# Expert loop of a 256-token mixture of experts on one core: the gather turned round, and TensorE's work behind the first layer in another order

## The reference, cut to what matters

```python
def moe_ffn(h, router_w, router_b, w1, b1, w2, b2):
    ...
    logits = (xt @ router_w + router_b).astype(jnp.float32)
    top_v, top_e = lax.top_k(logits, TOP_K)
    gate = jax.nn.softmax(top_v, axis=-1)
    ...
    def expert_block(args):
        rows, e = args
        xb = xt[rows]
        hb = xb @ w1[e] + b1[e]
        g, u = hb[:, :D_EXPERT], hb[:, D_EXPERT:]
        g = jnp.minimum(g, SWIGLU_LIMIT)
        u = jnp.clip(u, -SWIGLU_LIMIT, SWIGLU_LIMIT)
        glu = g * jax.nn.sigmoid(g * SWIGLU_ALPHA)
        return ((u + 1.0) * glu) @ w2[e] + b2[e]
    ...
    out = jnp.zeros((N, D), y.dtype).at[row_tok].add(y * row_w[:, None].astype(y.dtype))
```

## Time and profile before

| | us |
|---|---|
| Runs of the kernel before, three | 2416.95, 2409.55, 2408.04 |
| Their median | 2409.55 |
| Span of the profiled execution | 2412.2 |
| First-layer biases of expert 0 to the end of the last output sums | about 465 to 1620 |
| Main passes, further passes in it | 32, 2 |

### The profile page before, as it was taken

The page is one execution under the profiler, slowest core; times in us unless marked ns, Lnnn a source line. Parts: engine busy times, 40 slices in busy tenths (PEclk is TensorE's granted clock), DMA queues, the critical chain, the costliest instruction groups (busy, mean ns, idle before and its releaser), DMA issues.

```text
span 2412.2 us, 31828 instructions
## 1 busy us (share of the span) xinstructions
PE 2198.9 (91%) x11682; PEld 1314.5 (54%) x11683; DVE 723.1 (30%) x1577; ACT 476.3 (20%) x969; POOL 0.2 (0%) x4
## 2 busy tenths in 40 slices
PE   6999989788989988898988889989999999989997
PEld 3767756433333333333333333336648995756996
DVE  1313223211111111111111111121426772643776
ACT  1222230111001001111001100011224542113553
POOL 0000000000000000000000000000000000000000
PEclk9999989889999999999999999999999999999999
DMA  9234571789938999999999957985317655532662
GB/s 338 84 128 175 209 214 36 306 310 373 365 140 349 376 383 380 375 387 390 378 382 373 384 228 317 352 309 149 102 32 201 186 165 139 140 119 66 188 193 79
DMA packets 225825, 591.02 MB, mean 245 GB/s; under 512 B 14603, under 2 KB 114498, under 8 KB 189796
## 3 DMA queue, kind: packets, MB, share of 16 engines
q1 hardware_dynamic: 223804, 587.69, 67.5%
q10 hardware_dynamic: 1960, 2.46, 0.3%
HBM read 587.48 MB, written 2.62 MB: 245 GB/s over the span
## 4 chain that ended last, share of the span: by engine, by line
PE 89%; ACT 4%; DVE 3%; issue 2%; DMA 1%; SPq 0%; ACTq 0%; DVEq 0%
PE psum L1682 20%; PE psum L1700 12%; PE psum L1814 10%; PE psum L1350 7%; PE psum L1659 5%; PE psum L1826 5%; PE psum L1451 5%; PE psum L1456 4%; PE psum L1713 3%; PE psum L1483 2%; ACT upper L1132 2%; PE psum L1430 2%; PE psum L1676 2%; DMA lower<-in_mod_w 1%; PE psum L1436 1%
## 5 line engine op out<-in xcount | busy, mean ns | idle before, releaser
L1682 PE MATMUL psum<-lower,upper 128*64 128x512 f32 x2176 | 490.7, 609 | 0.0
L1682 PEld LDWEIGHTS psum<-lower,upper 128*64 128x64 f32 x2176 | 155.2, 139 | 334.9 <-issue 334.9
L1700 PE MATMUL psum<-upper 128*64 128x512 f32 x1088 | 279.0, 671 | 14.1 <-issue 12.7
L1814 PEld LDWEIGHTS psum<-rounded 128*128 128x128 f32 x2112 | 258.6, 189 | 3.4
L1814 PE MATMUL psum<-rounded 128*128 128x256 f32 x2112 | 260.1, 283 | 0.0
L2270 DVE TENSOR_SCALAR upper<-psum 128x512 f32<-128x512 f32 x34 | 23.5, 691 | 743.5 <-PE psum L1682 743.5
L1700 PEld LDWEIGHTS psum<-upper 128*64 128x64 f32 x1088 | 97.3, 153 | 169.0 <-issue 167.1
L1350 PE MATMUL psum<-upper,lower 128*128 128x256 f32 (+1 forms) x944 | 171.1, 383 | 1.4 <-DVE upper L1918 1.4
L1350 PEld LDWEIGHTS psum<-upper,lower 128*128 128x128 f32 (+1 forms) x944 | 133.8, 169 | 34.5 <-issue 8.5
L1138 ACT ACTIVATE upper<-upper 128x512 f32<-128x512 f32 x34 | 21.4, 629 | 599.5 <-DVE upper L2270 599.5
L1659 PEld LDWEIGHTS psum<-upper 128*128 128x128 f32 x1056 | 122.0, 194 | 27.8 <-issue 24.3
(11 more groups left out here) (365 smaller groups left out, 1827.9 us busy)
## 6 DMA issues: line engine op xcount, KB each, us to landing
lower<-in_exp_w SPq DMA_DIRECT2D x256, 1024.0 KB, 9.5
upper<-in_exp_w SPq DMA_DIRECT2D x256, 512.0 KB, 6.3
lower<-in_ffn_w_up SPq DMA_DIRECT2D x88, 512.0 KB, 5.4
lower<-in_mod_w SPq DMA_DIRECT2D x12, 2048.0 KB, 10.5
lower<-in_w_in SPq DMA_DIRECT2D x12, 2048.0 KB, 10.4
lower<-in_ffn_w_down SPq DMA_DIRECT2D x44, 512.0 KB, 5.7
lower<-in_odd_w_in SPq DMA_DIRECT2D x8, 2048.0 KB, 11.8
lower<-in_even_w_in SPq DMA_DIRECT2D x7, 2048.0 KB, 12.8
```

The lines of the kernel that those rows point to most:

```text
L1682: ins = pe.matmul(bank[4 + r // 2][64 * half:64 * half + 64], xg[:, k, 0:SLOTS], w1[k][:, 512 * r:512 * r + 512], start=False, stop=(n == ...
L1700: ins = pe.matmul(bank[6][64 * half:64 * half + 64], hiddenT[:, k % 4, 64 * (k // 4):64 * (k // 4) + 64], w2[k][:, 512 * half:512 * half + ...
L1814: ins = pe.matmul(bank[4 + b][:, T * g:T * g + T], w[:, g, k, :], x[:, k, :], start=(k == m == 0), stop=(k == KD - 1 and m == 2))
```

## The change

Ahead of the loop the scaled and shifted tokens `h2T` (features by tokens) are turned back into `h2` (tokens by features), which takes the place of `xn2`: 16 transposes on TensorE and four copies on ScalarE, and two busy-keeping matmuls in place of four. The gather takes the 64-column selection as stationary operand and `h2` as moving one: four matmuls of 512 columns, two column halves at a time, into bank 6. Its result is slots by features; ScalarE copies it to `xg` (one copy), four transposes (`turn_gathered`) put it into bank 7, and VectorE copies it to `xgT` (one copy). Scale and shift are in `h2` already, so the copies have none. `turn_hidden` of the main pass goes to bank 6.

On TensorE the order behind the first layer becomes: wait for `y_ready`; gather; spread out; (wait for the clipping) slot info; (wait for `xg`) turn hidden; turn gathered; output sums. The wait for `y_ready` at the head of an expert is gone. A further pass gathers from `h2`, and one VectorE copy replaces its multiply and add.

```diff
-        xgT = arena.take(1024, P)
+        xgT, xg = arena.take(512), arena.take(512)
...
-        select = arena.take(NT * P, P)
+        select = arena.take(NT * SLOTS, SLOTS)
...
+            for i in range(NT):
+                for half in range(2):
+                    act.wait_ge(x2_turned, 4 + 2 * i + half + 1)
+                    act.activation(h2[:, i, 512 * half:512 * half + 512], bank[2 + 2 * i + half],
+                                   ACT.Copy).then_inc(h2T_act, 1)
...
                 act.wait_ge(gathered, n)
-                for k in range(4):
-                    ins = act.activation(xgT[:, k, :], bank[7][:, P * k:P * k + P], ACT.Identity,
-                                         scale=scale2[:, k:k + 1], bias=mod[:, 24 + k:25 + k])
-                ins.then_inc(xg_lo, 1)
+                act.activation(xg, bank[6], ACT.Copy).then_inc(xg_copied, 1)
...
-            keep_busy(bank[7], 4)
+            for i in range(NT):
+                for half in range(2):
+                    for k in range(4):
+                        ins = pe.transpose(bank[2 + 2 * i + half][:, P * k:P * k + P],
+                                           h2T[:, 4 * half + k, P * i:P * i + P], ident)
+                    ins.then_inc(x2_turned, 1)
+            keep_busy(bank[7], 2)
...
             def gather(n):
                 pe.wait_ge(select_ready, n)
-                for k in range(KD):
-                    for i in range(NT):
-                        ins = pe.matmul(bank[7 - k // 4][:, P * (k % 4):P * (k % 4) + P], xn2[:, i, P * k:P * k + P],
-                                        select[:, i, :], start=(i == 0), stop=(i == NT - 1))
+                for i in range(NT):
+                    for half in range(2):
+                        ins = pe.matmul(bank[6][64 * half:64 * half + 64], select[:, i, :],
+                                        h2[:, i, 512 * half:512 * half + 512], start=(i == 0), stop=(i == NT - 1),
+                                        tile_position=(0, 64 * half))
                 ins.then_inc(gathered, 1)
+
+            def turn_gathered(n):
+                pe.wait_ge(xg_copied, n)
+                for j in range(4):
+                    ins = pe.transpose(bank[7][:, P * j:P * j + P], xg[:, P * j:P * j + P], ident)
+                ins.then_inc(xg_turned, 1)
...
-                pe.wait_ge(xg_lo, e + 1)
-                pe.wait_ge(xg_hi, e + 1)
+                pe.wait_ge(xgT_ready, e + 1)
                 pe.wait_ge(main_steps["slot_data"], e + 1)
-                if not first:
-                    pe.wait_ge(y_ready, e)
...
                 if not first:
+                    pe.wait_ge(y_ready, e)
+                gather(e + 2)
+                if not first:
                     pe.wait_ge(spread_ready, e)
                     spread_out(y_ready, e, spreadT, y_sb, spread_done)
-                gather(e + 2)
-                pe.wait_ge(xg_lo, e + 2)
-                turn_hidden(hidden_ready, e + 1, hidden_turned)
+                pe.wait_ge(main_steps["clipped"], e + 1)
                 slot_info(bank[5], select, info_done)
-                pe.wait_ge(xg_hi, e + 2)
+                pe.wait_ge(xg_copied, e + 2)
+                turn_hidden(bank[6], hidden_ready, e + 1, hidden_turned)
+                turn_gathered(e + 2)
                 output_sums(hiddenT_ready, e + 1, e, w2_used)
...
             def copy_gathered(n):
-                dve.wait_ge(gathered, n)
-                for k in range(4, KD):
-                    ins = dve.tensor_scalar(xgT[:, k, :], bank[6][:, P * (k - 4):P * (k - 4) + P], scale2[:, k:k + 1],
-                                            mod[:, 24 + k:25 + k], ALU.mult, ALU.add)
-                ins.then_inc(xg_hi, 1)
+                dve.wait_ge(xg_turned, n)
+                dve.tensor_copy(xgT, bank[7]).then_inc(xgT_ready, 1)
...
-                    dve.tensor_tensor(xgT_ov, bank[7].rearrange("p (k s) -> p k s", k=KD),
-                                      scale2.rearrange("p (k o) -> p k o", o=1).to_broadcast(wide),
-                                      ALU.mult).then_inc(more_steps["scaled"], 1)
-                    dve.wait_ge(more_steps["scaled"], n)
-                    dve.tensor_tensor(xgT_ov, xgT_ov, mod[:, 24:32].rearrange("p (k o) -> p k o", o=1).to_broadcast(wide),
-                                      ALU.add)
+                    dve.tensor_copy(xgT_ov.rearrange("p k s -> p (k s)"), bank[7])
...
                 make_select(e + 1, select_ready)
                 activation(w1_used, gate_ready, tanh_ready, hidden_ready, main_steps, e + 1, e * KD + KD)
-                copy_gathered(e + 2)
...
                 dve.tensor_copy(slot_data, bank[5][:, 0:2]).then_inc(main_steps["slot_data"], 1)
+                copy_gathered(e + 2)
```

More of the change, by code:

```diff
@@ L667, in program @@
         main_steps = {n: sem("dve_" + n) for n in ("clipped", "up_times_gate", "slot_data")}
-        more_steps = {n: sem("dve_more_" + n) for n in ("clipped", "up_times_gate", "slot_data", "scaled")}
+        more_steps = {n: sem("dve_more_" + n) for n in ("clipped", "up_times_gate", "slot_data")}
         moe_out_ready = sem("moe_out_ready")
@@ L1666, in slot_info, with hidden_sums @@
                     for i in range(NT):
-                        ins = pe.matmul(o[SLOTS * half:SLOTS * half + SLOTS, 0:2], sel[:, i, 0:SLOTS], expert_data[:, i, :],
+                        ins = pe.matmul(o[SLOTS * half:SLOTS * half + SLOTS, 0:2], sel[:, i, :], expert_data[:, i, :],
                                         start=(i == 0), stop=(i == NT - 1), tile_position=(0, SLOTS * half))
                 ins.then_inc(done, 1)
-            def hidden_sums(xg, e, used=None):
+            def hidden_sums(rows_of, e, used=None):
                 pe.wait_ge(b1_in, 16 * e + 16)
@@ L1681, in hidden_sums @@
                         half = r % 2
-                        ins = pe.matmul(bank[4 + r // 2][64 * half:64 * half + 64], xg[:, k, 0:SLOTS],
+                        ins = pe.matmul(bank[4 + r // 2][64 * half:64 * half + 64], rows_of(k),
                                         w1[k][:, 512 * r:512 * r + 512], start=False, stop=(n == KD - 1),
@@ L1687, in hidden_sums, with turn_hidden @@
                 return ins
-            def turn_hidden(ready, n, done):
+            def turn_hidden(o, ready, n, done):
                 pe.wait_ge(ready, n)
                 for j in range(4):
-                    ins = pe.transpose(bank[7][:, P * j:P * j + P], hidden[:, P * j:P * j + P], ident)
+                    ins = pe.transpose(o[:, P * j:P * j + P], hidden[:, P * j:P * j + P], ident)
                 ins.then_inc(done, 1)
@@ L1715, in spread_out, with gathered_rows @@
                 ins.then_inc(done, 1)
+            def gathered_rows(k):
+                at = P * (k % 4) + 64 * (k // 4)
+                return xgT[:, at:at + SLOTS]
             pe.wait_ge(route_ready, 1)
+            pe.wait_ge(h2T_act, 8)
             gather(1)
             slot_info(bank[5], select, info_done)
+            turn_gathered(1)
             def expert(e, first=False):
@@ L1735, in further_pass @@
                     pe.wait_ge(ov["select"], n)
+                    if p == 1 and not first:
+                        pe.wait_ge(y_ready, e)
                     for k in range(KD):
                         for i in range(NT):
-                            pe.matmul(bank[7][:, SLOTS * k:SLOTS * k + SLOTS], xn2[:, i, P * k:P * k + P],
+                            pe.matmul(bank[7][:, SLOTS * k:SLOTS * k + SLOTS], h2[:, i, P * k:P * k + P],
                                       select_ov[:, i, :], start=(i == 0), stop=(i == NT - 1))
@@ L1741, in further_pass @@
                     pe.wait_ge(ov["xg"], n)
-                    hidden_sums(xgT_ov, e).then_inc(ov["hidden"], 1)
-                    turn_hidden(ov["act"], n, ov["turned"])
+                    hidden_sums(lambda k: xgT_ov[:, k, :], e).then_inc(ov["hidden"], 1)
+                    turn_hidden(bank[7], ov["act"], n, ov["turned"])
                     output_sums(ov["copied"], n, e).then_inc(ov["y"], 1)
@@ L1753, in expert @@
                             further_pass(3)
-                hidden_sums(xgT, e, w1_used)
+                hidden_sums(gathered_rows, e, w1_used)
                 if first:
@@ L2259, in make_select @@
                     where = slot_of[:, i, 0:1] if isinstance(n, int) else slot_of[:, i, bass.ds(n, 1)]
-                    ins = dve.tensor_scalar(select[:, i, :], iota[:, 0:P], where, None, ALU.is_equal)
+                    ins = dve.tensor_scalar(select[:, i, :], iota[:, 0:SLOTS], where, None, ALU.is_equal)
                 ins.then_inc(done, 1)
```

15 lines of the change are left out of this document (8 added, 7 removed).

## The result

The changed kernel takes 2267.05 us (2265.0 to 2268.3, 4 runs) against 2410.68 (2408.04 to 2416.95, 4 runs): ratio 0.9385, 95% interval 0.9368 to 0.9402, 143.6 us less. The profiled executions have spans of 2266.4 and 2412.2.

What follows compares the result with a forecast made beforehand. TensorE's chain was taken to bound each period, with transfers at 30.2 us only 1.7 under the clean one. Savings of 3.1 + 20.3 + 1.5 + 79 + 20.2 = 124 from 2409.55 gave 2286 us (chance 0.50), range 2257 to 2335.

Steps and rivals of the forecast that it cites:

- Bound by TensorE before, by transfers in the middle after: Expert loop: TensorE's chain sets the old period; afterwards transfers of 30.2 us do in experts 6 to 26, saving 79.
- rival 1: Expert loop: TensorE sets the pace throughout and its clock stays up, 4.62 us saved a period, 2262 us; chance 0.22.
- Rival 2: Expert loads: transfers slower than the queued stretches say, floor 32.2 us a period, 2332 us; chance 0.20.
- rival 4: Expert loop: already transfer-bound, the gaps only show it, within 12 us of 2409; chance 0.04.
- Output sums at 20.3: Each period: output sums start 20.3 us after the biases in place of 23.65, 3.35 us saved.
- The wait at the head: Head of each expert: the 1.14 us gap is probably mostly the loop turn; 0 to 1.14 saved, 0.15 taken.
- The clock: Output sums: 1.12 us a pass lost to low clock behind idle time in front; half, 0.56, taken as saved.
- Two further passes: Further passes: one VectorE copy replaces two operations of 0.69 us, 1.5 us saved.
- Expert 0: Head of expert 1: TensorE idles until loads run out; without the thin stretch they end at 503.3, 3.1 us saved.
- rival 3: Heads of experts: a fetch stalls each loop turn under a never-empty queue, 6.8 us for 30 turns, 2490 us; chance 0.04.
- Ahead of the loop: Before expert 0: added transposes and smaller gather priced at nothing, covered by the loads' drain; otherwise up to 2 us either way.
- The tiling modes: TensorE's order: form changes four times a period, not three; a change costs at most 0.17 us, 5 us over 32 experts.

Runs made afterwards that it cites:

- 11: Changed kernel with chunks 4 to 7 of w2 loaded in 256 of 1024 columns, over all rows, from expert 1 on: 2222.36 us, ratio 0.9196.
- 1: Kernel before without the wait for `y_ready` at the head of an expert (kept only ahead of a further pass): 2341.84 us, ratio 0.9691.
- 3: Kernel before with two extra matmuls of 512 columns in the idle time between gather and transposes: 2412.50 us, ratio 0.9989.
- 7: Kernel before without the wait at the head, with 1.2 us of extra matmuls between spreading and gather: 2403.08 us, ratio 0.9951.
- 8: Changed kernel with the wait at the head put back and 2.13 us of extra matmuls ahead of slot info: 2340.65 us, ratio 0.9678.

## Why the prediction was right, and where it was off

- **Bound by TensorE before, by transfers in the middle after**: right, shown by 11 from the one side and by the waits from the other. The transfer period was put at 30.2; it is 30.16 to 30.31 once TensorE waits for weights. Experts 6 to 26 were to save 79 and saved 80. By the number alone rival 1 (2262, TensorE sets the pace throughout) lies nearer to 2267 than the 2286 did; its mechanism fell all the same, by the 59 waits for weights and by 11, which shows that TensorE alone would have given about 2222. Rival 2 needed a floor of 32.2, rival 4 no gain: both fell.
- **Output sums at 20.3**: 20.23. The gather took 1.89 (1.75), the transposes start 18.89 after the biases (19.0), and the four added transposes lie under ScalarE's copy. 3.42 saved, 3.35 said.
- **The wait at the head**: wrong. "I take 0.15, being nearest to VectorE's row": the gap went whole, 1.21, the upper bound and a little more (1). TensorE's loop turn lies beside its last output sums; VectorE's row of 1.88 says nothing of TensorE's.
- **The clock**: I took half of 1.12 a pass; nearly all came back (output sums 243.4 against 279.0, in the profile after). The reason I gave, idle time ahead of the output sums, was wrong as it stood: 3 filled it for nothing, and in 1 it stayed while the falls went. What decides is how the idle pieces recur (7, 8).
- These two terms make 1.06 + 0.56 = 1.6 us a period, 16 us over the ten experts outside the middle: periods of 27.25 where I had said about 29. Experts 1 to 5 had at least one fall each before, more than the mean that I used, which is most of the rest: 34.2 saved there and 28.5 in 27 to 31, where I had 20.3 (with 0.8 of the further pass) and 20.2. In the middle both terms were worth nothing, as the transfers set the end there; that is why the sum missed by no more than 20 us, 124 against 143.6.
- **Two further passes**: 1.5 said. The wait for VectorE at their heads fell from 2.14 and 2.13 to 1.41 and 1.39, 1.5 together.
- **Expert 0**: 3.1 said, 4.3 measured, and my reason does not hold as I put it. I read the idle time at the heads of experts 0 and 1 as a fetch that waits until the loads have run out. A fetch can be seen. In the trace of every kernel here one packet of the queue "instruction" lands ahead of TensorE's start at the heads of experts 0 and 1 and of the main pass of expert 6, and TensorE starts 1.5 to 1.8 us behind it; no other main pass has one in the 9 us ahead of its head. For expert 1, before (504 to 505.2, start at 506.61) and after (496.2 to 497.3, start at 498.81), queue, packets, MB, share:

```profile
q8 instruction: 1, 0.02, 5.4%
```
```profile
q8 instruction: 1, 0.02, 5.5%
```

- The trace does not name the engine that such a packet is for; that it is TensorE's is read from the times. It does not wait for the loads to run out, as it lands while they still run (after, they end at about 501). At expert 1 it starts 1.0 to 2.3 behind the last output sums in the kernels without the wait at the head, and 4.3 to 4.6 in those with it; the idle time there is 3.5 to 4.8 and 6.8 to 8.6. So 2.0 of the 4.3 came with the wait's removal and 2.3 with the shorter chain. That the 4.3 are near the 3.1 is partly luck: the kernel of 11, with the same work of TensorE in expert 0, took 42.33 for it at a clock of 0.78, against 37.40 at 0.91. Only the head of expert 6 had such a packet behind these two, with 1.9 us idle before and 1.6 after, so rival 3 fell.
- **Ahead of the loop**: nothing said, for the drain of the loads as cover. That reading fails too: expert 0 starts 1.5 behind its packet, 6.4 to 7.5 behind TensorE's last work, in every kernel. What the change is worth there cannot be told from the scatter between executions.
- **The tiling modes**: gather to spreading is 1.82 and spreading to slot info 1.92, each for work of 1.75, so a change of mode cost at most 0.1 and 0.2, and the output sums still started at 20.23.
- Lost, and not predicted: 2.9 in the second further pass. Its output sums ran at half clock, 9.48 in place of 7.09; the same pass takes 30.6 to 35.0 in the other traces, so no run ties the loss to the change.

## What to carry to other kernels

Before an idle stretch is filled or a wait is priced by its own length, look at how the idle pieces recur: 1.2 us of work more in a period (7) cost some 20 us of clock here, and 2.3 us more (8) gave about as much back. A wait that stands earlier than its data is needed is worth taking out even where another engine's row suggests that it is hidden, and it costs two lines to try. When a loop's chain comes within a few us of its transfers, work out how many periods the loads are ahead: that number, not the mean bandwidth, says, beside the rate with queued loads, how much of the gain survives.

## What was not expected of the hardware

A wait of 1.14 us cost 2.3 us a period (73 us over the loop), about half of it through the clock. The same idle time per period left the clock up at 30.7 us a period and lowered it in 13 of 21 at 31.9. The core's loads ran at 417 GB/s for 422 us without a thin stretch. TensorE's starts at the heads of experts 0, 1 and 6 stood 1.5 to 1.8 us behind a packet of the instruction queue in all fourteen traces.
